# The delta rule's diagonal blocks inverted whole on GpSimd, in a fused transformer block and gMLP mixer

## Chip, cores and metric

One core of a Trainium2 chip. The metric is the device time of one execution in microseconds; of several executions, the median. The engines: TensorE (PE) multiplies, VectorE (DVE), ScalarE (ACT) and GpSimd (POOL) work element by element, and SyncE (SP) issues the transfers. TensorE writes to PSUM banks, the other data lie in SBUF.

## What is computed

Batch 1, 256 tokens, width 2048, all in float32. The first block has a modulation by `w_ada`, an input projection, a latent attention of 8 heads, a gated delta rule of 8 heads of 128, output projections and a gated feed-forward part of width 5632. A second block is a gMLP mixer of width 4096, with a norm at the end. The change is in the delta rule, which the reference computes in chunks of 64 tokens:

```python
kb = k * beta[..., None]
Lmat = jnp.where(strict, jnp.einsum('bhncd,bhnsd->bhncs', kb, k) * decay, 0.0)
A = Lmat + jnp.eye(CHUNK, dtype=jnp.float32)
rhs = jnp.concatenate([v * beta[..., None], kb * jnp.exp(G)[..., None]], axis=-1)
sol = lax.linalg.triangular_solve(A, rhs, left_side=True, lower=True, unit_diagonal=True)
```

The solution gives `u` and `w`; a scan over the chunks carries the state S of each head and yields the outputs. The kernel takes chunks of 128 tokens, so there are two for each head, and it needs to apply the inverse of a unit lower triangular matrix of 128 x 128 for each head and chunk.

## The kernel before

**A list of slots.** `Schedule` writes one list of steps, and each engine's program goes through that list and issues its own part, in order. The products of the weights are jobs of 512 output columns: TensorE consumes their weights in halves of two blocks of 128 rows, 12 products of 128x512 each, because every weight is split into a high and a low part (`hi` by ScalarE's cast, line 1528, `lo` by DVE's subtraction, line 2080) and each product is made of three. A half needs a place in SBUF for its two parts; four places serve this section (`NHL`), and a place is free once TensorE has consumed the half in it (`free_place`, `fill`). After each half `slot()` lets every background generator take one step. So a generator that yields n times spreads its steps over n slots.

**The section around the change.** It is the list of jobs `b`: for each c of 4 the pair `ga` (8 halves) and `om` (4), then `z` (2 jobs of 8) and `gb` (4 of 8). Beside them the remaining rows of `w_ada` come in by the units of `BESIDE`, and DVE reduces them, one row sum of 128x1024 each (line 2067). In this section `cells()` starts the delta rule: `prepare` for two chunks (tt) and two groups of four heads (g), then `invert`, then `solve(0, g)` and behind it `solve(1, g)`, then `gdn_final`. `build()` asks after the jobs of `b` for `("ogdn", 1, 1)`, the last transposes of `gdn_final`; if they had not been reached, slots without products would follow. In the list of before, the old inversion starts in slot 76 (`inv_in`), its eight slots of steps are 77 to 84, `inv_x` and `inv_out` stand in 85 and 86, the cells in 88 to 119, the last `og_t` in 132, and the last half of `gb` in 143. A step stands in front of the half of its slot: slot 90 opens with the first `ZT`, then comes its half.

**The inversion.** The strictly lower part of each 128x128 matrix (`Lm`, transposed) has four diagonal blocks of 32, each again of two by two blocks of 16. ScalarE picks the diagonal blocks (`gdn_pick`, line 1715) into `LP`. On DVE, `inv_in` (line 2293) transposes blocks of 32x32, and keeps for each partition the 16 entries of its own block of 16 (`LB`, with `bm2` as masks). `inv` (lines 2308 and 2311) does 15 steps j, a product and an addition over (15-j) x (j+1) columns each, all 128 partitions at once: the 16x16 blocks inverted. `inv_x` on ScalarE (line 1723) spreads them with the masks in two forms, `inv_out` (line 2316) transposes both back: `XO[0]` and `XO[1]`, the block inverses X and their transposes XT. Every one of these waits on semaphore `inv` or `gdn_pick`.

**The cells.** `dve_cell` in step X spreads the blocks into `X` and `XT` (line 2579), and for chunk 0 scales k (line 2613). Then TensorE multiplies `Lm` with `XT` (step ZT, four products of 128x128 in fp32 by `each`, line 1445), DVE masks the result with `pair` (line 2616), TensorE multiplies `X` with it (XZ), and DVE adds it to `XT` (line 2621): now XT holds the transposed inverses of the 32x32 blocks. Step NT multiplies once more and masks with `off`; U, NU, NW and NY apply the rest of the inverse. X, ZT, XZ and NT take two slots each.

**GpSimd** has nothing but powers: `power` (line 2669) forms x to the -0.5 for the norms, on 1, 2 or 4 columns. Each waits for its argument from DVE (line 1964).

Of the kernel before, what the change touches and what calls it, by code (L numbers as in the profile page):

```python
# [21 lines left out]
C_ID, C_ONE, C_INV, C_NH, C_COL, C_POS, C_C, C_TRI, C_PAIR = 0, 128, 256, 288, 296, 552, 554, 576, 704  # L22
C_OFF, C_CM, C_BM, C_ID16, C_AL, C_DT, C_GN, C_END = 832, 960, 1088, 1096, 1352, 1360, 1368, 1496
# [6 lines left out]
def shape_constants():  # L30
    i = np.arange(P)
    row, col = i[:, None], i[None, :]
    c = np.zeros((P, C_END), np.float32)
    c[:, C_ID:C_ID + P] = np.eye(P)
    c[:, C_ONE:C_ONE + P] = 1.0
    c[:, C_TRI:C_TRI + P] = row <= col
    c[:, C_PAIR:C_PAIR + P] = (row // 32 == col // 32) & (row % 32 < 16) & (col % 32 >= 16)
# [119 lines left out]
class Layout:  # L157


    def __init__(self, nc):  # L160
# [29 lines left out]
        self.pair, self.off, self.bm2 = C[:, C_PAIR:C_PAIR + P], C[:, C_OFF:C_OFF + P], C[:, C_BM:C_BM + 2]  # L190
# [62 lines left out]
        def pairs(kb):  # L253
            return ar(kb, 512).rearrange("p (j b n) -> p j b n", b=2, n=16)
        self.LP, self.LT = pairs(40), pairs(42)
        self.LB, self.XB, self.XP = (ar(kb, 256).rearrange("p (i j) -> p i j", j=16) for kb in (44, 45, 46))
        self.XE = [pairs(48), pairs(50)]
        self.XO = [ar(kb, 512).rearrange("p (n c) -> p n c", c=32) for kb in (12, 14)]
# [71 lines left out]
GATES = {"gta": 32, "gtf": 80}  # L330

# [5 lines left out]
class Schedule:  # L337
# [545 lines left out]
    def invert(self):  # L883
        while not {("prep", tt, g) for tt in range(2) for g in range(2)} <= self.have:
            yield
        yield
        self.put("inv_in")
        yield
        for j in range(0, 15, 2):
            self.put("inv", j, j + 2)  # L890
            yield
        self.put("inv_x")
        yield
        self.put("inv_out")
# [177 lines left out]
def cell_values(part, tt):  # L1072
    if part == 0:
        return (["kT", "qT", "KK", "AT"], ["d", "dm", "L", "Lb", "at", "atm"], ["kT", "exp", "qT"])
    if tt == 0:
        return (["ZT", "XZ", "NT", "U", "NU", "NW", "NY", "o", "S"],
                ["X", "XT", "kd", "ZT", "R", "XT2", "NT", "W", "V", "S", "ss", "n1", "n2"], ["U", "Y", "o", "sq"])
    return (["ZT", "XZ", "NT", "kS", "qS", "U", "NU", "NW", "NY", "o"],
            ["X", "XT", "ZT", "XT2", "NT", "R1", "R2", "R3", "QS", "W", "V", "o", "ss", "n1", "n2"], ["U", "Y", "sq"])
# [342 lines left out]
def pe_cell(e, L, S, W, held, args):  # L1422
# [42 lines left out]
    elif name == "ZT":  # L1465
# [37 lines left out]
def act_program(e, L, S, sch):  # L1503
# [3 lines left out]
    for step in sch.steps:  # L1507
# [200 lines left out]
        elif kind == "gdn_pick":  # L1708
# [249 lines left out]
def dve_program(e, L, S, sch):  # L1958
# [74 lines left out]
    for step in sch.steps:  # L2033
# [256 lines left out]
        elif kind == "inv_in":  # L2290
            W.wait_ge("gdn_pick", 16)
            W.wait_ge("cst_in", 32)
            e.transpose(L.LT.rearrange("p j b n -> p (j b n)"), L.LP.rearrange("p j b n -> p (j b n)")).then_inc(S["inv"], 1)
            lb = L.LB.rearrange("p i j -> p j i")
            W.wait_ge("inv", 1)
            e.tensor_scalar(lb, L.LT[:, :, 0, :], L.bm2[:, 0:1], None, ALU.mult).then_inc(S["inv"], 1)
            e.tensor_tensor(L.XB, L.CID, L.CID, ALU.mult).then_inc(S["inv"], 1)
            W.wait_ge("inv", 2)
            e.scalar_tensor_tensor(out=lb, in0=L.LT[:, :, 1, :], scalar=L.bm2[:, 1:2], in1=lb, op0=ALU.mult, op1=ALU.add
                                   ).then_inc(S["inv"], 1)  # L2300

        elif kind == "inv":
            j0, j1 = args
            for j in range(j0, min(j1, 15)):
                rows, shape = L.XB[:, j + 1:16, 0:j + 1], [P, 15 - j, j + 1]
                t = L.XP[:, 0:15 - j, 0:j + 1]
                W.wait_ge("inv", 2 * j + 4)
                e.tensor_tensor(t, L.LB[:, j + 1:16, j:j + 1].to_broadcast(shape),
                                L.XB[:, j:j + 1, 0:j + 1].to_broadcast(shape), ALU.mult).then_inc(S["inv"], 1)
                W.wait_ge("inv", 2 * j + 5)  # L2310
                e.tensor_tensor(rows, rows, t, ALU.add).then_inc(S["inv"], 1)
# [246 lines left out]
def dve_cell(e, L, S, W, args, mean_eps):  # L2558
# [104 lines left out]
def pool_program(e, L, S, sch):  # L2663
# [7 lines left out]
    for step in sch.steps:  # L2671
# [201 lines left out]
```

## Time and profile before

| | us |
|---|---|
| median of 3 runs | 2217.33 |
| lowest, highest | 2216.49, 2218.11 |
| profiled execution, first to last instruction | 2215.9 |
| PE busy in it | 2178.7 |
| DVE busy | 1499.2 |
| ACT busy | 1004.1 |
| POOL busy | 25.4 |

No time of its own beyond the span is listed for the profiled execution; the median is 1.4 us above that span. The granted clock of TensorE is 0.995 of full speed over the span and 1.00 in the windows of the section. Busy times of PE are modelled: a product of 128x512 is shown with 0.39 us, though the next one starts 0.23 us behind it, so starts are compared, not durations. On DVE consecutive records overlap by about 0.08 us. Idle time stands in brackets with what ended it. The lines named are those of the kernel before.

### The profile page before, as it was taken

Reading aid. Unit: us, or ns where it says so; the run is one execution under the profiler, and the core shown is the slowest. Engines: PE = TensorE matmul, PEld = TensorE weight load, DVE = VectorE, ACT = ScalarE, POOL = GpSimd, SP = SyncE. Lnnn points to the kernel's source line nnn. Section 1 sums busy time; section 2 is a strip of 40 time slices with the busy share of each in tenths; the row PEclk is TensorE's granted clock in tenths of the full one; section 3 lists DMA queues with packets and bytes.
Section 4 is the critical chain, followed back from the end, with each engine's and each line's share of the span. In section 5 each row is a group of like instructions: output and inputs, shape, how many; then the busy total and the mean of one; then the engine's idle time right before and its main releaser. Section 6 shows DMA issues by size and latency. Waiting matters only on the chain.

```text
span 2215.9 us, 27209 instructions
## 1 busy us (share of the span) xinstructions
PE 2178.7 (98%) x10552; PEld 1830.3 (83%) x10552; DVE 1499.2 (68%) x1881; ACT 1004.1 (45%) x1286; POOL 25.4 (1%) x26
## 2 busy tenths in 40 slices
PE   6899999999999999999999999999999999999998
PEld 5789988888888888888888888888888888888887
DVE  8988698988888677755455555575546555655556
ACT  5357455433444644443444334465444444444444
POOL 0001000000000000000000000000000000000000
PEclk9999999999999999999999999999999999999999
DMA  9975568977998688866666666666666666666663
GB/s 404 420 275 166 186 220 279 305 244 245 331 337 302 207 277 292 295 219 191 192 191 186 191 197 190 187 203 192 190 197 185 191 194 191 189 192 189 194 190 128
DMA packets 241552, 507.08 MB, mean 229 GB/s; under 512 B 19304, under 2 KB 34960, under 8 KB 235920
## 3 DMA queue, kind: packets, MB, share of 16 engines
q1 hardware_dynamic: 241424, 505.35, 70.2%
q8 instruction: 83, 1.36, 0.2%
q14 instruction: 45, 0.37, 0.0%
HBM read 503.16 MB, written 2.12 MB: 228 GB/s over the span
## 4 chain that ended last, share of the span: by engine, by line
PE 86%; DVE 6%; DMA 4%; ACT 2%; issue 2%; POOL 0%; DVEq 0%; ACTq 0%; POOLq 0%
PE bank L1254 25%; PE bank L1256 25%; PE bank L1255 25%; DVE WL L2080 2%; PE bank L1445 2%; PE bank L1186 2%; PE bank L1261 1%; PE bank L1263 1%; PE bank L1262 1%; DVE RAW L2067 1%; ACT WH L1528 1%; DMA RAW<-in_w_cd_dram 1%; DMA RAW<-in_w_ada_dram 1%; DMA A<-in_w_cq_dram 1%; DMA RAW<-in_w_cq_dram 1%
## 5 line engine op out<-in xcount | busy, mean ns | idle before, releaser
L2080 DVE TENSOR_TENSOR WL<-RAW,WH 128x1024 fp32r<-128x1024 f32 x706 | 859.9, 1222 | 576.7 <-ACT WH L1528 567.3
L1528 ACT CAST WH<-RAW 128x1024 fp32r<-128x1024 f32 x706 | 738.4, 1049 | 849.1 <-PE bank L1256 702.0
L1254 PE MATMUL bank<-WH,HTh 128*128 128x512 f32 x1922 | 758.1, 394 | 1.1 <-DVE WL L2080 1.0
L1256 PE MATMUL bank<-WH,HTl 128*128 128x512 f32 x1922 | 749.1, 390 | 0.0
L1255 PE MATMUL bank<-WL,HTh 128*128 128x512 f32 x1922 | 748.4, 389 | 0.0
L1256 PEld LDWEIGHTS bank<-WH,HTl 128*128 128x128 f32 x1922 | 360.8, 188 | 76.2
L1254 PEld LDWEIGHTS bank<-WH,HTh 128*128 128x128 f32 x1922 | 361.1, 188 | 75.7 <-DVE WL L2080 2.4
L1255 PEld LDWEIGHTS bank<-WL,HTh 128*128 128x128 f32 x1922 | 361.2, 188 | 72.2
L1254 PE MATMUL bank<-WH,R2h 128*128 128x512 f32 x408 | 160.6, 394 | 0.3 <-DVE WL L2080 0.3
L1256 PE MATMUL bank<-WH,R2l 128*128 128x512 f32 x408 | 159.0, 390 | 0.0
L1255 PE MATMUL bank<-WL,R2h 128*128 128x512 f32 x408 | 158.9, 389 | 0.0
L1254 PE MATMUL bank<-WH,aTh 128*128 128x512 f32 x344 | 134.1, 390 | 0.0
L1256 PE MATMUL bank<-WH,aTl 128*128 128x512 f32 x344 | 133.9, 389 | 0.0
L1255 PE MATMUL bank<-WL,aTh 128*128 128x512 f32 x344 | 133.8, 389 | 0.0
L2067 DVE CUSTOM_DVE_ANT_0 RAW<-RAW,CB,CST 128x1024 f32<-128x1024 f32 (+1 forms) x79 | 116.8, 1479 | 0.3
L1254 PEld LDWEIGHTS bank<-WH,R2h 128*128 128x128 f32 x408 | 76.6, 188 | 16.2 <-DVE WL L2080 0.8
L1256 PEld LDWEIGHTS bank<-WH,R2l 128*128 128x128 f32 x408 | 76.6, 188 | 16.1
L1255 PEld LDWEIGHTS bank<-WL,R2h 128*128 128x128 f32 x408 | 76.7, 188 | 15.4
L1261 PE MATMUL bank<-HTh,WH 128*128 128x256 f32 x308 | 89.4, 290 | 0.0
L1263 PE MATMUL bank<-HTh,WL 128*128 128x256 f32 x308 | 87.1, 283 | 0.0
L1262 PE MATMUL bank<-HTl,WH 128*128 128x256 f32 x308 | 87.1, 283 | 0.0
L2067 DVE CUSTOM_DVE_ANT_0 RAW<-RAW,CB,MOD 128x1024 f32<-128x1024 f32 x64 | 81.7, 1277 | 0.0
(302 smaller groups left out, 1823.5 us busy)
## 6 DMA issues: line engine op xcount, KB each, us to landing
RAW<-in_a_w_in_dram SPq DMA_DIRECT2D x192, 512.0 KB, 4.2
RAW<-in_w_gate_up_dram SPq DMA_DIRECT2D x176, 512.0 KB, 4.5
RAW<-in_w_ada_dram SPq DMA_DIRECT2D x128, 512.0 KB, 5.5
RAW<-in_w_in_dram SPq DMA_DIRECT2D x112, 512.0 KB, 4.8
RAW<-in_w_down_dram SPq DMA_DIRECT2D x88, 512.0 KB, 4.3
RAW<-in_a_w_out_dram SPq DMA_DIRECT2D x64, 512.0 KB, 4.1
A<-in_w_ada_dram SPq DMA_DIRECT2D x17, 1024.0 KB, 14.0
RAW<-in_w_o_dram SPq DMA_DIRECT2D x32, 512.0 KB, 5.9
```

What stands on the lines that cost most here:

```text
L1186: t = e.transpose(dst[:, i * P:(i + 1) * P], s, ident)
L1254: e.matmul(o, ah[:, s], hi[:, k, :], start=first, stop=False)
L1255: e.matmul(o, ah[:, s], lo[:, k, :], start=False, stop=False)
L1256: i = e.matmul(o, al[:, s], hi[:, k, :], start=False, stop=last)
L1261: e.matmul(o, hi[:, k, s], ah, start=first and cb % 2 == 0, stop=False, skip_group_check=True)
L1262: e.matmul(o, hi[:, k, s], al, start=False, stop=False, skip_group_check=True)
L1263: i = e.matmul(o, lo[:, k, s], ah, start=False, stop=last, skip_group_check=True)
L1445: i = e.matmul(dst[:, h, :], left[:, h, :], right[:, h, :], start=True, stop=True)
L1528: e.copy(hi, rv).then_inc(S["hi"], 1)
L2067: e.tensor_tensor_reduce(out=rv, in0=rv, in1=L.CB[:, w], scale=0.5, scalar=first[:, col:col + 1], op0=ALU.mult, op1=ALU.add, accum_out=L.M ...
L2080: e.tensor_tensor(lo, rv, hi.bitcast(F32), ALU.subtract).then_inc(S["lo"], 1)
```

## The change

The diagonal blocks of 32 are inverted whole, in 31 steps over up to 16 columns a partition (the two halves of a block's columns lie in different partitions), and GpSimd does these steps instead of DVE. `inv` now has 62 instructions, each waiting for the one before. For them there are 13 slots (`INV_STEPS`) and six empty ones. The steps ZT and XZ with their products, masks and additions are gone, and so is the block form `XO[0]`: step X spreads only `XT`. `v` is scaled in step X. The inversion runs through larger picks and transposes, and `XO` is the sum of the two halves of `XF`. The constant `pair` is gone, which makes the constants 128 columns shorter.

```diff
+INV_STEPS = [(0, 3), (3, 6)] + [(j, j + 2) for j in range(6, 24, 2)] + [(24, 27), (27, 31)]
@@ invert
-        for j in range(0, 15, 2):
-            self.put("inv", j, j + 2)
+        for j0, j1 in INV_STEPS:
+            self.put("inv", j0, j1)
+            yield
+        for _ in range(6):
             yield
@@ solve
-        for name in ("X", "ZT", "XZ", "NT") + ("kS",) * tt + ("U", "NU", "NW", "NY", "o"):
+        for name in ("X", "NT") + ("kS",) * tt + ("U", "NU", "NW", "NY", "o"):
             at(name)
             yield
-            if name in ("X", "ZT", "XZ", "NT"):
+            if name in ("X", "NT"):
                 yield
@@ pe_cell
-    elif name == "ZT":
+    elif name == "NT":
         for n in (na, nb):
             for other, value in held[n]:
                 W.wait_ge(other, value)
         W.wait_ge(dve, d("XT"))
-        each(a, Lm, XT).then_inc(mine, 1)
-    elif name == "XZ":
-        W.wait_ge(dve, d("ZT"))
-        each(b, X, q).then_inc(mine, 1)
-    elif name == "NT":
-        W.wait_ge(dve, d("XT2"))
         each(a, Lm, XT).then_inc(mine, 1)
@@ act_program
                 e.copy(L.LP[r, :, :, n:n + 4].rearrange("p j b h -> p h b j"),
-                       lm[r, :, r].rearrange("p h (b j) -> p h b j", j=16)).then_inc(S["gdn_pick"], 1)
+                       lm[r, :, r].unsqueeze(2).to_broadcast([32, 4, 2, 32])).then_inc(S["gdn_pick"], 1)
         elif kind == "inv_x":
-            W.wait_ge("inv", 34)
-            for n in range(2):
-                src = L.XB if n else L.XB.rearrange("p i j -> p j i")
-                for b in range(2):
-                    e.activation(L.XE[n][:, :, b, :], src, ACT.Copy, scale=L.bm2[:, b:b + 1]).then_inc(S["gdn_pick"], 1)
+            W.wait_ge("inv", 65)
+            for b in range(2):
+                e.activation(L.XE[:, :, b, :], L.XB, ACT.Copy, scale=L.bm2[:, b:b + 1]).then_inc(S["gdn_pick"], 1)
@@ dve_program
-            e.transpose(L.LT.rearrange("p j b n -> p (j b n)"), L.LP.rearrange("p j b n -> p (j b n)")).then_inc(S["inv"], 1)
...
+            e.transpose(L.LT.rearrange("p j i -> p (j i)"), L.LP.rearrange("p j b n -> p (j b n)")).then_inc(S["inv"], 1)
+            for b in range(2):
+                e.tensor_scalar(L.XB[:, 16 * b:16 * b + 16, :], L.CID, L.bm2[:, b:b + 1], None, ALU.mult).then_inc(S["inv"], 1)
         elif kind == "inv_out":
-            for n in range(2):
-                W.wait_ge("gdn_pick", 2 * n + 18)
-                e.transpose(L.XO[n].rearrange("p n (b j) -> p j b n", b=2), L.XE[n]
-                            ).then_inc(S["inv"], 1)
+            W.wait_ge("gdn_pick", 18)
+            e.transpose(L.XF.rearrange("p i b n -> p (i b n)"), L.XE.rearrange("p i b c -> p (i b c)")).then_inc(S["inv"], 1)
+            W.wait_ge("inv", 66)
+            e.tensor_tensor(L.XO.rearrange("p n i -> p i n"), L.XF[:, :, 0, :], L.XF[:, :, 1, :], ALU.add).then_inc(S["inv"], 1)
@@ dve_cell
-        spread_blocks(X, L.XO[0])
-        spread_blocks(XT, L.XO[1])
+        spread_blocks(XT, L.XO)
         if tt == 0:
             e.tensor_tensor(k, k, bc4(L.eD[:, 0, hs]), ALU.mult).then_inc(mine, 1)
-    elif name == "ZT":
-        W.wait_ge(pe, m("ZT"))
-        e.tensor_tensor(q, a, bm4(L.pair), ALU.mult).then_inc(mine, 1)
-        if tt == 0:
             e.tensor_tensor(v, v, bc4(L.beta[:, 0, hs]), ALU.mult).then_inc(mine, 1)
-    elif name == "XZ":
-        W.wait_ge(pe, m("XZ"))
-        e.tensor_tensor(XT, XT, b, ALU.add).then_inc(mine, 1)
@@ pool_program
+        elif kind == "inv":
+            for j in range(*args):
+                n, w = 31 - j, min(j + 1, 16)
+                rows, t, shape = L.XB[:, j + 1:32, 0:w], L.XP.rearrange("p i c -> p (i c)")[:, 0:n * w], [P, n, w]
+                t = t.rearrange("p (i c) -> p i c", c=w)
+                W.wait_ge("inv", 2 * j + 3)
+                e.tensor_tensor(t, L.LT[:, j, j + 1:32].unsqueeze(2).to_broadcast(shape),
+                                L.XB[:, j:j + 1, 0:w].to_broadcast(shape), ALU.mult).then_inc(S["inv"], 1)
+                W.wait_ge("inv", 2 * j + 4)
+                e.tensor_tensor(rows, rows, t, ALU.add).then_inc(S["inv"], 1)
```

## Rows read from the trace of the kernel before

**Rows 1.** The page: span, busy time by engine (us, share), chain by engine.
```profile
span 2215.9 us, 27209 instructions
...
PE 2178.7 (98%) x10552; PEld 1830.3 (83%) x10552; DVE 1499.2 (68%) x1881; ACT 1004.1 (45%) x1286; POOL 25.4 (1%) x26
...
PE 86%; DVE 6%; DMA 4%; ACT 2%; issue 2%; POOL 0%; DVEq 0%; ACTq 0%; POOLq 0%
```

**Rows 2.** Windows: us, then busy us (instructions) by engine, clock, DMA share, GB/s.
```profile
390.00:400.00 10.00, 10.00 (x46) 8.29 (x45) 9.96 (x16) 4.26 (x6) 0.00 (x0) 1.00 0.86 272
410.00:420.00 10.00, 10.00 (x46) 8.29 (x45) 9.62 (x23) 3.96 (x4) 0.00 (x0) 1.00 1.01 355
420.00:430.00 10.00, 9.92 (x44) 7.87 (x44) 9.97 (x16) 6.35 (x9) 0.00 (x0) 1.00 0.91 301
430.00:440.00 10.00, 9.46 (x50) 7.80 (x49) 10.00 (x15) 3.00 (x3) 0.00 (x0) 1.00 0.83 284
```

**Rows 3.** Timeline of PE: start us, us, engine, line, operation, count [idle before].
```profile
432.71 0.39 PE L1256 MATMUL bank<-WH,HTl 128*128 128x512 f32 x1
432.94 0.39 PE L1254 MATMUL bank<-WH,HTh 128*128 128x512 f32 x1
...
434.32 1.13 PE L1445 MATMUL bank<-A 128*128 128x128 f32 x8 [0.54 <-DVE A L2579]
...
437.80 0.39 PE L1256 MATMUL bank<-WH,HTl 128*128 128x512 f32 x1
438.02 1.05 PE L1445 MATMUL bank<-A 128*128 128x128 f32 x8
438.83 0.48 PE L1254 MATMUL bank<-WH,HTh 128*128 128x512 f32 x1
439.15 0.40 PE L1255 MATMUL bank<-WL,HTh 128*128 128x512 f32 x1
```

**Rows 4.** Timeline of DVE, first and last step of the old inversion.
```profile
397.09 0.70 DVE L2293 STREAM_TRANSPOSE A<-A 128x512 f32<-128x512 f32 x1
...
427.49 2.11 DVE L2316 STREAM_TRANSPOSE A<-A 128x512 f32<-128x512 f32 x2
```

**Rows 5.** Lines of DVE, 399 to 448.5: count | busy us, mean ns.
```profile
L2080 DVE TENSOR_TENSOR WL<-RAW,WH 128x1024 fp32r<-128x1024 f32 x16 | 19.5, 1216 | 0.0
...
L2579 DVE TENSOR_TENSOR A<-A,CST 128x512 f32<-128x512 f32 x4 | 2.6, 681 | 0.0
...
L2311 DVE TENSOR_TENSOR A<-A 128x63 f32<-128x63 f32 x2 | 0.5, 225 | 0.1
```

**Rows 6.** Timeline of POOL, powers of one and four columns.
```profile
485.98 1.95 POOL L2669 TENSOR_TENSOR ST<-ST,CST 128x4 f32<-128x4 f32 x1 [4.84 <-DVE ST L1964]
543.10 1.01 POOL L2669 TENSOR_TENSOR ST<-ST,CST 128x4 f32<-128x4 f32 x1 [55.17 <-DVE ST L1964]
...
745.37 0.55 POOL L2669 TENSOR_TENSOR ST<-ST,CST 128x1 f32<-128x1 f32 x1 [195.26 <-DVE ST L1964]
```

**Rows 7.** Timeline of DVE beside the power at 485.98.
```profile
485.84 1.22 DVE L2080 TENSOR_TENSOR WL<-RAW,WH 128x1024 fp32r<-128x1024 f32 x1
```

**Rows 8.** Timeline of both engines, 304 to 307.
```profile
304.05 2.70 POOL L2669 TENSOR_TENSOR ST<-ST,CST 128x4 f32<-128x4 f32 x2 [93.13 <-DVE ST L1964]
...
304.67 1.22 DVE L2264 SCALAR_TENSOR_TENSOR A<-A 128x1024 f32<-128x1024 f32 x1
...
305.81 1.28 DVE L2067 CUSTOM_DVE_ANT_0 RAW<-RAW,CB,MOD 128x1024 f32<-128x1024 f32 x1
...
307.01 1.22 DVE L2080 TENSOR_TENSOR WL<-RAW,WH 128x1024 fp32r<-128x1024 f32 x1
```

**Rows 9.** Lines of ACT, 399 to 448.5: count | busy us, mean ns | idle before.
```profile
L1528 ACT CAST WH<-RAW 128x1024 fp32r<-128x1024 f32 x16 | 16.7, 1050 | 26.5 <-DMA RAW<-in_w_o_mla_dram 18.5 <-DMA RAW<-in_w_in_dram 8.1
L1723 ACT ACTIVATE A<-A,CST 128x256 f32<-128x256 f32 x4 | 2.2, 622 | 1.6 <-DVE A L2311 1.6
L1747 ACT ACTIVATE A<-bank 128x512 f32<-128x512 f32 x4 | 2.2, 591 | 0.1
```

More of the change, by code:

```diff
@@ L20 @@
 KB = 256
-C_ID, C_ONE, C_INV, C_NH, C_COL, C_POS, C_C, C_TRI, C_PAIR = 0, 128, 256, 288, 296, 552, 554, 576, 704
-C_OFF, C_CM, C_BM, C_ID16, C_AL, C_DT, C_GN, C_END = 832, 960, 1088, 1096, 1352, 1360, 1368, 1496
+C_ID, C_ONE, C_INV, C_NH, C_COL, C_POS, C_C, C_TRI = 0, 128, 256, 288, 296, 552, 554, 576
+C_OFF, C_CM, C_BM, C_ID16, C_AL, C_DT, C_GN, C_END = 704, 832, 960, 968, 1224, 1232, 1240, 1368
 CS = 3 * P + 80
@@ L36, in shape_constants @@
     c[:, C_TRI:C_TRI + P] = row <= col
-    c[:, C_PAIR:C_PAIR + P] = (row // 32 == col // 32) & (row % 32 < 16) & (col % 32 >= 16)
     c[:, C_OFF:C_OFF + P] = row // 32 < col // 32
@@ L189, in __init__ @@
         self.CID = C[:, C_ID16:C_ID16 + 256].rearrange("p (i j) -> p i j", j=16)
-        self.pair, self.off, self.bm2 = C[:, C_PAIR:C_PAIR + P], C[:, C_OFF:C_OFF + P], C[:, C_BM:C_BM + 2]
+        self.off, self.bm2 = C[:, C_OFF:C_OFF + P], C[:, C_BM:C_BM + 2]
         self.bm4 = C[:, C_BM + 2:C_BM + 6]
@@ L252, in __init__ @@
         self.SS = [ar(96, 512).rearrange("p (h d) -> p h d", d=P), ar(98, 512).rearrange("p (h d) -> p h d", d=P)]
[L253 to L258, printed above, removed]
+        self.LP = ar(40, 1024).rearrange("p (j b n) -> p j b n", b=2, n=16)
+        self.LT = ar(44, 1024).rearrange("p (j i) -> p j i", i=32)
+        self.XB, self.XP = (ar(kb, w).rearrange("p (i c) -> p i c", c=16) for kb, w in ((48, 512), (50, 256)))
+        self.XE = ar(52, 1024).rearrange("p (i b c) -> p i b c", b=2, c=16)
+        self.XF = ar(40, 1024).rearrange("p (i b n) -> p i b n", b=2, n=16)
+        self.XO = ar(12, 512).rearrange("p (n i) -> p n i", i=32)
         self.cell = [[ar(64 + 16 * g + 2 * i, 512).rearrange("p (h d) -> p h d", d=P) for i in range(8)] for g in range(2)]
@@ L1075, in cell_values @@
     if tt == 0:
[L1076 to L1079, printed above, removed]
+        return (["NT", "U", "NU", "NW", "NY", "o", "S"],
+                ["XT", "kd", "R", "NT", "W", "V", "S", "ss", "n1", "n2"], ["U", "Y", "o", "sq"])
+    return (["NT", "kS", "qS", "U", "NU", "NW", "NY", "o"],
+            ["XT", "NT", "R1", "R2", "R3", "QS", "W", "V", "o", "ss", "n1", "n2"], ["U", "Y", "sq"])
 def count_cells():
@@ L2292, in dve_program @@
             W.wait_ge("cst_in", 32)
-            e.transpose(L.LT.rearrange("p j b n -> p (j b n)"), L.LP.rearrange("p j b n -> p (j b n)")).then_inc(S["inv"], 1)
[L2294 to L2299, printed above, removed]
-                                   ).then_inc(S["inv"], 1)
[L2302 to L2311, printed above, removed]
+            e.transpose(L.LT.rearrange("p j i -> p (j i)"), L.LP.rearrange("p j b n -> p (j b n)")).then_inc(S["inv"], 1)
+            for b in range(2):
+                e.tensor_scalar(L.XB[:, 16 * b:16 * b + 16, :], L.CID, L.bm2[:, b:b + 1], None, ALU.mult).then_inc(S["inv"], 1)
         elif kind == "inv_out":
-            for n in range(2):
-                W.wait_ge("gdn_pick", 2 * n + 18)
-                e.transpose(L.XO[n].rearrange("p n (b j) -> p j b n", b=2), L.XE[n]
-                            ).then_inc(S["inv"], 1)
+            W.wait_ge("gdn_pick", 18)
+            e.transpose(L.XF.rearrange("p i b n -> p (i b n)"), L.XE.rearrange("p i b c -> p (i b c)")).then_inc(S["inv"], 1)
+            W.wait_ge("inv", 66)
+            e.tensor_tensor(L.XO.rearrange("p n i -> p i n"), L.XF[:, :, 0, :], L.XF[:, :, 1, :], ALU.add).then_inc(S["inv"], 1)
         elif kind == "z":
@@ L2607, in dve_cell @@
     elif name == "X":
-        W.wait_ge("inv", 36)
+        W.wait_ge("inv", 67)
         W.wait_ge(own, CELL["dve", 1, "atm"] if tt == 0 else CELL["dve", 0, "n2"])
-        spread_blocks(X, L.XO[0])
-        spread_blocks(XT, L.XO[1])
+        spread_blocks(XT, L.XO)
         if tt == 0:
             e.tensor_tensor(k, k, bc4(L.eD[:, 0, hs]), ALU.mult).then_inc(mine, 1)
-    elif name == "ZT":
-        W.wait_ge(pe, m("ZT"))
-        e.tensor_tensor(q, a, bm4(L.pair), ALU.mult).then_inc(mine, 1)
-        if tt == 0:
             e.tensor_tensor(v, v, bc4(L.beta[:, 0, hs]), ALU.mult).then_inc(mine, 1)
-    elif name == "XZ":
-        W.wait_ge(pe, m("XZ"))
-        e.tensor_tensor(XT, XT, b, ALU.add).then_inc(mine, 1)
     elif name == "NT":
```

## The prediction, before the changed kernel was timed

> **What bounds the kernel now.** I read the page first. TensorE is busy for 2178.7 of the 2215.9 us of the span and holds 86% of the chain that ended last, and VectorE (DVE) is second [rows 1]. So what comes off TensorE's queue comes off the time, and what makes TensorE wait is added. GpSimd (POOL) is free: 25.4 us in the whole span. Then I read the windows around the inversion, which DVE's timeline starts at 397.09 [rows 4]. There DVE is full too: 9.6 to 10 us of every 10 from 390 to 440, with TensorE losing only 0.08 and 0.54 us between 420 and 440 [rows 2]. The program is a list of slots; in each, TensorE consumes one half of weights, 12 products. In TensorE's timeline they start 0.227 us apart (432.71 to 432.94, rounded) [rows 3], so a slot is 2.72 us of TensorE. Counting the schedule, the old inversion begins in slot 76 and its `inv_out` stands in slot 86; DVE takes 30.4 us for these ten slots (397.09 to 427.49) [rows 4] where TensorE needs 27.2. DVE's lead is eaten here, and only four halves can be prepared ahead.
>
> All costs come from one profiled execution of 2215.9 us span. No time of its own outside the span is listed; the runs' median is 2217.33, 1.4 us more, and I carry differences over to that median. A measurement of this kernel can tell about 0.2% (4.4 us) from no change.
>
> **TensorE, removed.** `ZT` and `XZ` each issue four products in fp32, 8 records, for each of four cells: eight groups. From a product at 437.80, the next one after such a group starts at 438.83 instead of 438.02: 0.81 us. The first product behind it then takes 0.32 us to its successor (438.83 to 439.15) instead of 0.227: 0.09 more [rows 3]. Eight times 0.90 is **7.2 us**. They stand alone in their slots, so the switch is paid for each. The wait of 0.54 us in front of the first group (434.32, behind the spreading of X) [rows 3] and the 0.08 us before it [rows 2] come from DVE being late; with DVE relieved I take **0.6 us** as gone. Together 7.8 us, 2209.5, if nothing else waits.
>
> **Slots.** The inversion gets 13 slots of steps and 6 empty ones for 8: eleven more. Each cell drops four, and two cells follow one another: eight fewer. The last cell transposes move from slot 132 to 135, and the section ends with slot 143, so no slot without products appears: 0 us, covered by 12 slots of slack (past it, each extra one would be a bubble of the chain's length).
>
> **DVE.** Gone are 30 small operations of up to 0.225 us (at most 6.8 us), and in the four cells a spread, a mask and an addition of 0.68 each (8.2 us) [rows 5]. The doubled block transpose in front costs 0.7 us more; behind, one of twice the width plus an addition takes the place of two of together 2.11 us [rows 4]: even. All of it lies beside TensorE; it is only worth the 0.6 us above. **ScalarE**: the 16 picks copy 256 instead of 128 values; `inv_x` is two operations of 512 columns for four of 0.62 us [rows 9]. The first costs less than 0.2 us each, beside ScalarE's waits for DMA (26.5 us of idle time in 49.5) [rows 9]: 0; without that cover 3 us. Constants: 64 KB less in one early transfer, 0.
>
> **GpSimd, added.** 62 dependent products and additions with 9552 columns in all (the sum of (31-j) times min(j+1,16), twice). No row shows one of them. The nearest on the same engine are powers: 0.55 us for one column, 1.01 for four [rows 6], thus 0.40 fixed and 0.153 per column. The nearest of the same kind is DVE's: 0.682 for 512 columns, 1.216 for 1024 [rows 5], 1.04 ns a column. So 62 x 0.40 = 24.5 us (DVE's own fixed part, 0.15 us, would give 9), and for the columns between 9.9 us and, at the power's rate, 1461 us. A multiplication is one pass and no power, so I stay near DVE's row; since POOL's fixed part is 2.6 times DVE's, I take twice its rate, 2.06 ns, 19.7 us. Alone the chain takes **44.2 us**. The Trainium skill (GPSIMD Engine Reference, Performance versus the Vector engine) has 4497 ns for 2048 columns; by that, an estimate from the page, the columns come to 21 us and nothing else changes.
>
> **Does it fit?** DVE ends the new `inv_in` near 399.2 (1.4 us of transposing, then two small ones). `inv_x` opens slot 96 on ScalarE, behind the cast of slot 95. The group that opened slot 90 could start at 433.6 without its wait; the place which that cast fills comes free five halves later, 433.6 + 5 x 2.72 = 447.2, and the cast of 1.05 us [rows 9] ends at 448.2. That gives 49 us. Alone, POOL ends at 443.4: in time, by 5 us.
>
> But POOL isn't alone. A power of four columns takes 1.01 us beside a DVE operation with one input in SBUF, and 1.95 when it starts (485.98) behind a DVE subtraction with both inputs in SBUF (485.84, 1.22 us): it ends 0.87 us after that one [rows 6, 7]. The same pair stands at 548. In [rows 8] the second of two powers runs only behind 304.67 + 1.22 and ends 0.86 us later, though DVE's next operation had already begun: POOL gets in between two of them, once. The Trainium skill (SBUF — State Buffer, Who interferes with whom) says that such a DVE instruction and a GpSimd instruction that reads SBUF exclude each other, the later one waiting to the end; the trace agrees (1.95 against 1.01).
>
> In the 49 us DVE does 18 splits, which hold it for 1.14 us each (304.67 to 305.81, an operation of the same 1.22), and, by the units planned beside these jobs, 15 row sums of `ada`, 1.20 each (305.81 to 307.01) [rows 8]: 38.5 us with both inputs in SBUF, 78%. The open 11 us are about what the readings at the seams take (33 x 0.32). So POOL does about one instruction per DVE instruction, 34 of 62, until 448.2. The last 28 (columns 17 to 30) have 3360 columns: 11.1 + 6.9 = 18 us, now unhindered, since DVE soon waits for ScalarE, which waits at `inv_x`. POOL ends at **466.5**.
>
> **What is queued behind.** Behind `inv_x` on ScalarE stand the casts, behind them DVE's splits, and TensorE has four more halves ready, until 433.6 + 9 x 2.72 = 458.1. The next one is there at 466.5 + 1.2 (`inv_x`, 2 x 0.59) + 1.05 + 1.22 = 470.0: TensorE stands for 11.9 us. With no lead left, DVE then needs 4.4 us for the next slot (`inv_out` 2.1, a row sum, a split) against 2.72, and 3.8 in each slot that begins a cell (three operations of 0.68 less 0.08 of overlap, a split, three quarters of a row sum): 1.7 + 2.2. The stall is **15.8 us**, the sum -7.2 - 0.6 + 15.8 = **+8.0 us: 2225.3**.
>
> **Rivals.**
> A. The chain fits (faster). If POOL and DVE pass each other more easily than [rows 7] say, or POOL's fixed part is DVE's, it ends before 454.7 (458.1 - 3.4), which is 0.90 us per instruction. Then only the 7.8 us count: 2209.5. For it: alone it needs 0.71 us each. Against: both stretched powers. Chance 0.33. With 3.9 us of catching up behind it, break-even is a stall of 7.8 us, at 0.96 us each.
> B. Half a lock (even). If `ada`'s row sums don't hold POOL up (no row shows that they do), only 20 of the 49 us are closed; POOL ends between 455 and 462, the stall is 3 to 11 us: 2213 to 2221. Chance 0.13.
> C. DVE is held too, for as long as POOL reads. 34 instructions with 6192 columns x 2.06 ns would add 12.8 us to DVE's 41 (38.5 and two evictions of two operations) in those 49 us, 4.6 us too much: 2230; with twice the time per column, 6.9 us more behind the window and some in it, about 2240. For it: one shared way in works both ways. Against: no DVE operation in the rows is stretched (those powers read only a few columns). Chance 0.19. The Trainium skill (SBUF — State Buffer, Who interferes with whom) states this direction too; no row shows it.
> D. Multiplications cost what powers do: over 3600 us. Chance 0.01.
> Forecast: 0.34.
>
> **How the numbers follow.** Faster by over 0.2%: A, and a sliver of B: 0.34. Within: the rest of B, 0.13. Slower: forecast, C and D, 0.53. The range runs from just under A (2208.5) to the upper end of C (2240). The forecast's own range is 2221 to 2230.
>
> **What would show it.** L1445 with 64 fewer records. POOL at some 40 to 60 us busy from 399 on, its operations stretched where they meet L2080 and L2067; DVE rows of these lines longer than 1.22 and 1.28 would be C. Idle time of ScalarE at `inv_x` behind POOL, and TensorE idle for 10 to 20 us between 455 and 490. If POOL ends before 450 and TensorE has no such gap, the step of the shared way was wrong and A holds.

## The result, and the profile after

The changed kernel takes **2221.93 us** (median of 10 runs, 2221.51 to 2223.48) against 2217.16 (10 runs, 2215.79 to 2218.11): the ratio is 1.0022, interval 1.0015 to 1.003, thus 4.8 us slower (3.3 to 6.6). Forecast were 2225.3 and a range of 2208.5 to 2240. The page of the profile after, against [rows 1]:

```profile
span 2221.4 us, 27098 instructions
...
PE 2174.5 (98%) x10488; PEld 1825.4 (82%) x10488; DVE 1497.9 (67%) x1838; ACT 1011.4 (46%) x1284; POOL 86.6 (4%) x88
...
PE 86%; DVE 5%; DMA 3%; POOL 3%; ACT 2%; issue 1%; DVEq 0%; ACTq 0%; POOLq 0%
```

TensorE has 64 records and 4.2 us of work less, and yet the span is 5.5 us longer. GpSimd works 61.2 us more, and it now has 3% of the chain that ended last, where it had nothing. The windows around the inversion, with the columns of [rows 2], show where TensorE's gain was given back:

```profile
430.00:440.00 10.00, 10.00 (x46) 8.29 (x45) 10.00 (x10) 2.12 (x2) 9.53 (x7) 1.00 0.90 306
440.00:450.00 10.00, 9.99 (x45) 7.94 (x44) 10.00 (x11) 5.20 (x6) 9.53 (x7) 1.00 0.99 354
450.00:460.00 10.00, 8.37 (x36) 6.56 (x36) 7.16 (x9) 1.05 (x1) 9.14 (x12) 1.00 0.94 319
460.00:470.00 10.00, 0.77 (x2) 0.67 (x3) 2.05 (x2) 4.42 (x6) 4.45 (x15) 0.68 0.04 15
470.00:480.00 10.00, 10.00 (x42) 8.19 (x41) 9.97 (x14) 1.76 (x2) 0.00 (x0) 0.81 0.70 221
```

Between 430 and 440 TensorE no longer loses the 0.54 us of [rows 2]; between 460 and 470 it does next to nothing, and the granted clock is 0.68. Who waited for whom between 390 and 560 (waiter, releaser: us in total, times, longest us):

```profile
ACT A L1717 <- POOL A L2670: 14.3, 1, 14.3
...
PE bank L1256 <- DVE WL L2074: 10.9, 1, 10.9
...
DVE WL L2074 <- ACT WH L1524: 15.6, 6, 10.8
...
PE bank L1447 <- DVE A L2603: 0.7, 1, 0.7
```

So it is the forecast's queue: GpSimd's last addition (L2670) releases `inv_x` on ScalarE (L1717), the cast behind it (L1524) releases DVE's split (L2074), and that releases TensorE. The same chain in the timelines of GpSimd, ScalarE and DVE:

```profile
399.64 1.15 POOL L2667 TENSOR_TENSOR A<-A 128x31 f32<-128x31 f32 x1 [92.72 <-DVE A L2289]
...
420.97 0.57 POOL L2667 TENSOR_TENSOR A<-A 128x220 f32<-128x220 f32 x1
...
439.27 1.49 POOL L2667 TENSOR_TENSOR A<-A 128x256 f32<-128x256 f32 x1
...
440.83 1.60 POOL L2670 TENSOR_TENSOR A<-A 128x256 f32<-128x256 f32 x1
...
458.16 0.43 POOL L2667 TENSOR_TENSOR A<-A 128x144 f32<-128x144 f32 x1
...
465.33 0.22 POOL L2670 TENSOR_TENSOR A<-A 128x16 f32<-128x16 f32 x1
```

```profile
450.26 1.05 ACT L1524 CAST WH<-RAW 128x1024 fp32r<-128x1024 f32 x1 [1.56 <-DMA RAW<-in_w_in_dram]
465.58 1.34 ACT L1717 ACTIVATE A<-A,CST 128x512 f32<-128x512 f32 x2 [14.27 <-POOL A L2670]
466.82 3.88 ACT L1524 CAST WH<-RAW 128x1024 fp32r<-128x1024 f32 x4
```

```profile
420.34 1.27 DVE L2328 SCALAR_TENSOR_TENSOR A<-A,bank 128x512 f32<-128x512 f32 x2
...
438.57 1.70 DVE L2074 TENSOR_TENSOR WL<-RAW,WH 128x1024 fp32r<-128x1024 f32 x1
440.20 1.64 DVE L2061 CUSTOM_DVE_ANT_0 RAW<-RAW,CB,MOD 128x1024 f32<-128x1024 f32 x1
...
467.95 1.23 DVE L2074 TENSOR_TENSOR WL<-RAW,WH 128x1024 fp32r<-128x1024 f32 x1 [10.79 <-ACT WH L1524]
469.10 1.24 DVE L2293 STREAM_TRANSPOSE A<-A 128x1024 f32<-128x1024 f32 x1
470.37 1.07 DVE L2295 TENSOR_TENSOR A<-A 128x512 f32<-128x512 f32 x1
```

From 399.64 to 465.55 are 65.9 us for 62 dependent instructions. The first, of 31 columns, takes 1.15 us. The two of 256 columns at 439.27 and 440.83 take 1.49 and 1.60 us and start 1.56 us apart, beside DVE operations of 1.70 and 1.64 us that start 1.63 apart: the two engines go at one pace, while the same two DVE operations take 1.22 and 1.28 where nothing meets them. Later (458.16), with DVE waiting for ScalarE, a product of 144 columns takes 0.43 us. Nor does every DVE operation hold GpSimd up: beside L2328 (420.34), which reads one of its inputs from a bank in PSUM, the product of 220 columns at 420.97 takes 0.57 us, and beside the same line at 454.33 a product of 176 columns takes 0.48 (454.95), which is its length alone (445.90 in the first run below). TensorE's timeline:

```profile
457.99 0.39 PE L1258 MATMUL bank<-WH,HTl 128*128 128x512 f32 x1
469.23 0.79 PE L1256 MATMUL bank<-WH,HTh 128*128 128x512 f32 x1 [10.86 <-DVE WL L2074]
469.82 0.63 PE L1257 MATMUL bank<-WL,HTh 128*128 128x512 f32 x1
470.25 0.63 PE L1258 MATMUL bank<-WH,HTl 128*128 128x512 f32 x1
...
474.00 0.39 PE L1258 MATMUL bank<-WH,HTl 128*128 128x512 f32 x1
474.24 0.39 PE L1256 MATMUL bank<-WH,HTh 128*128 128x512 f32 x1
```

It would have gone on at 458.2 (457.99 + 0.227) and does so at 469.23: 11.0 us. The 12 products of this half then take until 474.24, 5.0 us instead of 2.72. They start 0.43 us apart (469.82 to 470.25), 1.9 times the 0.227 of full speed, which is the level of 1.2 GHz; from 474.00 on they are back at 0.24. The low clock costs 2.3 us more.

### The profile page after: what moved, and what is told of

Same layout as the page of the kernel before. It is cut to its first block, busy times and chain, and to the rows that moved or that the text cites. A ratio compares the mean times of both kernels' runs of the same rounds, so it can differ in the third digit from the quotient of the medians.

```text
span 2221.4 us, 27098 instructions
## 1 busy us (share of the span) xinstructions
PE 2174.5 (98%) x10488; PEld 1825.4 (82%) x10488; DVE 1497.9 (67%) x1838; ACT 1011.4 (46%) x1284; POOL 86.6 (4%) x88
## 3 DMA queue, kind: packets, MB, share of 16 engines
q8 instruction: 83, 1.36, 0.2%
## 4 chain that ended last, share of the span: by engine, by line
PE 86%; DVE 5%; DMA 3%; POOL 3%; ACT 2%; issue 1%; DVEq 0%; ACTq 0%; POOLq 0%
PE bank L1256 26%; PE bank L1258 26%; PE bank L1257 25%; DVE WL L2074 2%; PE bank L1188 2%; POOL A L2670 1%; PE bank L1263 1%; PE bank L1265 1%; PE bank L1264 1%; POOL A L2667 1%; PE bank L1447 1%; DVE RAW L2061 1%; ACT WH L1524 1%; DMA RAW<-in_w_cd_dram 1%; DMA RAW<-in_w_ada_dram 1%
## 5 line engine op out<-in xcount | busy, mean ns | idle before, releaser
L2074 DVE TENSOR_TENSOR WL<-RAW,WH 128x1024 fp32r<-128x1024 f32 x706 | 866.5, 1232 | 584.6 <-ACT WH L1524 576.8
L1524 ACT CAST WH<-RAW 128x1024 fp32r<-128x1024 f32 x706 | 741.5, 1054 | 833.6 <-PE bank L1258 684.6
```

Source lines behind the costliest of these rows:

```text
L1524: e.copy(hi, rv).then_inc(S["hi"], 1)
L2074: e.tensor_tensor(lo, rv, hi.bitcast(F32), ALU.subtract).then_inc(S["lo"], 1)
```

## The experiments

Two theories stood against each other at first. **P**: the shared way of the forecast (one GpSimd instruction per two-input DVE operation). **Q**: GpSimd's instructions are slow in themselves. Then came the questions of what removes the stall, and what the removed products were worth. Each time stands beside that of the kernel before, timed together with it; "ends" is the end of GpSimd's last addition.

**1 to 3: how many slots are kept for the chain.** The changed kernel has `range(6)`.

```diff
-        for _ in range(6):
+        for _ in range(0):    # e1; 10 in e2, 13 in e3
```

> The changed kernel with none of the six empty slots. ScalarE then reaches inv_x six slots (16.3 us of TensorE) earlier, near 435 instead of 451.3, and TensorE runs dry near 442 instead of 458.2. Theory P (GpSimd is held up by DVE's operations with two inputs in SBUF, and runs free once DVE stands): about 35 of the 62 instructions are still to do at 436, with some 4860 columns; at the free rate of the changed kernel's rows (0.27 us each and 1.7 ns a column) they take 18 us, the chain ends near 455 instead of 465.5, the stall grows only from 11 to about 16 us: 2227.5 us. Rival Q (GpSimd's own pace, DVE has no part): the chain ends at 465.5 as before, the stall grows by the whole 16.3 us: 2238 us.

> The changed kernel with ten empty slots instead of six; TensorE needs the next half 10.9 us later, near 469. Rival Q (GpSimd's own pace): the chain ends at 465.5, its followers 3.7 us later, so TensorE hardly waits: 2210 us, all of the 7.8 us gained. Theory P (held up by DVE): DVE goes on for four more slots, the tail of the chain that ran free now meets it too, at 1.1 to 1.4 us an instruction; the chain ends between 467 and 470, and a stall of 2 to 5 us with its low clock remains: 2212 to 2215 us.

> Thirteen empty slots; the last cell transposes then stand in slot 142, just ahead of the end of the section in 143. Both theories: no stall is left, since even with every instruction held up (62 times 1.4 us at most, less for the short ones) the chain ends before TensorE needs its half near 477. 2209 to 2211 us: the eight groups of products (7.2 us) and the small waits, so this run prices the removed products. If TensorE's gain was less than 0.9 us a group, it shows here.

| slots kept | ends (us) | TensorE's wait (us) | time, before (us) | ratio (interval) |
|---|---|---|---|---|
| 0 | 455.6 | 18.4 | 2230.02, 2217.53 | 1.0057 (1.0043 to 1.0071) |
| 6 (the change) | 465.6 | 10.9 | 2221.93, 2217.16 | 1.0022 (1.0015 to 1.003) |
| 10 | 472.7 | 6.9 | 2218.91, 2217.53 | 1.0007 (0.9998 to 1.0016) |
| 13 | 476.2 | 2.9 + 1.1 | 2215.89, 2217.53 | 0.9992 (0.9983 to 1.0) |

GpSimd's timeline without the slots:

```profile
434.32 1.48 POOL L2667 TENSOR_TENSOR A<-A 128x252 f32<-128x252 f32 x1
...
435.88 1.55 POOL L2670 TENSOR_TENSOR A<-A 128x252 f32<-128x252 f32 x1
...
438.99 0.62 POOL L2667 TENSOR_TENSOR A<-A 128x256 f32<-128x256 f32 x1
...
439.69 0.74 POOL L2670 TENSOR_TENSOR A<-A 128x256 f32<-128x256 f32 x1
...
455.42 0.22 POOL L2670 TENSOR_TENSOR A<-A 128x16 f32<-128x16 f32 x1
```

With `inv_x` earlier in its queue, DVE runs out of splits earlier (its last operation before the stall starts at 436.81), GpSimd is alone from 437.5 on, and its operations fall from 1.55 to 0.62 and 0.74 us. The chain ends 10 us earlier at the same count and size of instructions, so P holds and Q does not. The end was expected near 455 and came at 455.6; the stall of 18.4 us was expected at about 16, and the time is 2.5 us over the 2227.5 expected. The stall is longer than with six slots, since TensorE ran dry earlier. More slots are each worth less than the 2.72 us of TensorE that they give, because the chain gets longer in them. In the run with ten:

```profile
464.04 1.36 POOL L2670 TENSOR_TENSOR A<-A 128x144 f32<-128x144 f32 x1
...
466.81 0.46 POOL L2670 TENSOR_TENSOR A<-A 128x128 f32<-128x128 f32 x1
...
472.44 0.22 POOL L2670 TENSOR_TENSOR A<-A 128x16 f32<-128x16 f32 x1
```

Even the addition of 144 columns is still held to 1.36 us; it goes free only at 466.8. From 0 to 6, 10 and 13 slots the end moves by 10.0, 7.1 and 3.5 us, for 16.3, 10.9 and 8.2 us of TensorE's work. My expectations for ten and thirteen failed: the times came 4 to 7 us later, since they let the tail run free, and for thirteen slots they had no stall at all. They also left out the clock. TensorE with thirteen slots:

```profile
479.90 0.50 PE L1256 MATMUL bank<-WH,HTh 128*128 128x512 f32 x1 [2.93 <-DVE WL L2074]
...
480.99 0.63 PE L1256 MATMUL bank<-WH,HTh 128*128 128x512 f32 x1
481.42 0.63 PE L1257 MATMUL bank<-WL,HTh 128*128 128x512 f32 x1
```

After a wait of only 2.9 us products again start 0.43 us apart, and the 12 of this half take 4.4 us instead of 2.72 (the last one starts at 484.11): 1.7 us more. With ten slots it is 2.0 us (476.38 to 481.06) behind a wait of 6.9, with six 2.3 behind 11.0. So the price of the low clock hardly followed the length of the wait in these three runs. For thirteen slots the terms are 7.9 us gained (below), 4.0 of waits and 1.7 of clock: 2.2 us faster, and 1.6 was measured.

**4: the same inversion on DVE.** The block `inv` goes from `pool_program` to `dve_program`, its 62 operations unchanged.

```diff
@@ pool_program
-        elif kind == "inv":
@@ dve_program
+        elif kind == "inv":
```

> The changed kernel, but VectorE does the 62 steps itself, in the same slots. GpSimd has nothing. VectorE's own cost is 62 times 0.2 us and 9552 columns at 1.04 ns: 22 us more work for it in 19 slots (52 us of TensorE), where it has about 44 us already: 66 against 52, less a lead of 4 us: TensorE waits for about 8 to 10 us, in small pieces: 2218 to 2221 us. If the chain on GpSimd cost nothing but its own time, this would be the slower one; if sharing the way in costs DVE as much as doing the work (its operations grew from 1.22 to 1.7 us), they are about equal.

2221.01 us (before 2217.53), 1.0017 (1.0008 to 1.0026): at the upper end of what was expected, and within the intervals the same as on GpSimd (1.0022, 1.0015 to 1.003). In DVE's timeline a step of 256 columns takes 0.42 us, less than on GpSimd alone (0.62 and 0.74):

```profile
422.67 0.42 DVE L2297 TENSOR_TENSOR A<-A 128x256 f32<-128x256 f32 x1
```

The time is lost in another way, mostly in small waits of TensorE (380 to 600: waiter, releaser, total, times, longest):

```profile
PE bank L1256 <- DVE WL L2074: 7.6, 7, 2.1
```

Between 400 and 450 TensorE is busy for 43.14 us of 50 here, where the changed kernel has 49.99. So with these slots handing the chain to the idle engine bought nothing over leaving it on DVE: there its 62 operations make DVE late in many places, on GpSimd they make one long wait. DVE's version with fewer empty slots was not tried; it may not need the six.

**5 and 6: columns or count.** Both leave out a part of the inversion, so their results are not the inverse, and each was timed once. The first leaves out half of the columns of each step; the second leaves out all 31 additions.

```diff
# e5
-                n, w = 31 - j, min(j + 1, 16)
+                n, w = 31 - j, (min(j + 1, 16) + 1) // 2
# e6 (waits of inv: j + 3, 34, 35, 36)
-                W.wait_ge("inv", 2 * j + 4)
-                e.tensor_tensor(rows, rows, t, ALU.add).then_inc(S["inv"], 1)
```

> The changed kernel, each of the 62 GpSimd instructions on about half the columns (4968 instead of 9552 in all; the other half is left out). Theory P (each instruction waits for one DVE operation with two inputs in SBUF, so their count sets the end): the middle ones shrink only by their own reading, from 1.55 to 1.35 us, and the chain ends near 459 instead of 465.5. DVE's splits beside them, 1.70 us with full columns, shrink to about 1.45, halfway to 1.22. Rival (the columns set the end): 66 us become about 40, the chain ends near 440.

> The changed kernel without the 31 additions on GpSimd (they are left out, so the chain has 31 instructions with 4776 columns, about as many columns as the run before it). Theory P: 31 instructions at 1.35 us end near 441, some 18 us before the chain with half the columns. Rival (columns set the end): both end at the same time, near 440. TensorE has no stall here in either case: about 2210 to 2212 us, and the profile shows what is left of the gain when only DVE's slower operations remain.

Both leave GpSimd about half of the 9552 columns (4968 and 4776). With half the width the chain runs from 397.9 to 455.4, 57.5 us (its end was expected near 459), TensorE still waits once for 2.5 us, and the kernel takes 2212.74 us (before 2217.38). GpSimd, and the DVE operation beside it:

```profile
431.37 1.27 POOL L2667 TENSOR_TENSOR A<-A 128x128 f32<-128x128 f32 x1
```

```profile
433.65 1.46 DVE L2074 TENSOR_TENSOR WL<-RAW,WH 128x1024 fp32r<-128x1024 f32 x1
```

With half the instructions it takes 41.7 us and ends at 439.2 (expected near 441), with no stall, 2208.13 us (expected 2210 to 2212). The group of all 31 in GpSimd's timeline:

```profile
397.49 41.73 POOL L2667 TENSOR_TENSOR A<-A 128x31 f32<-128x31 f32 x31 [91.98 <-DVE A L2289]
```

At equal columns the count makes 16 us of difference, 1.35 us per instruction against 0.93. Halving the columns took 8.4 us off the 65.9, halving the count 24.2. The number of turns weighs most, as P says; the columns count too, since they make each turn longer. The split's length follows the columns beside it: 1.22 us beside none, 1.46 beside 128, 1.70 beside 255.

**7: what the removed products were worth.** The kernel before gets eight more groups of four products, in the slots behind the steps ZT and NT.

```diff
+                if name in ("ZT", "NT"):
+                    at("more")
...
+    elif name == "more":
+        each(b, Lm, XT)
```

> The kernel before, with one more group of four products of 128x128 alone in each of eight slots, into a bank that is free (its result isn't used). It prices the removed products: eight groups at 0.90 us are 7.2 us: 2224.7 us. If a group cost only the 0.53 us that its eight records would take at the pace of the big products in columns, it would be 2221.5 us; if TensorE had room, 2217.5.

2223.39 us against 2217.38, 1.003 (1.0018 to 1.0041): 6.0 us (4.0 to 9.1), 7.2 expected. TensorE's timeline shows two groups back to back:

```profile
437.52 0.39 PE L1258 MATMUL bank<-WH,HTl 128*128 128x512 f32 x1
...
437.75 1.95 PE L1447 MATMUL bank<-A 128*128 128x128 f32 x16
...
439.45 0.48 PE L1256 MATMUL bank<-WH,HTh 128*128 128x512 f32 x1
```

From 437.75 to 439.45 are 1.70 us for two groups where [rows 3] have 0.81 for one: the second adds 0.89. Eight are 7.1 us. The expectation was wrong in one thing: none of the eight stands alone in its slot, each joins a group that was there. So the run prices a second group (0.89), and the price of one that stands alone, as the removed ones did, remains that of [rows 3] (0.81 + 0.09); the two are equal to 0.01 us. The time agrees, but by itself it can't tell them from the rival of 0.53 us a group (4.2 us), which lies in its interval too; the rows can.

**8 to 10: fewer row sums beside the chain.** If DVE's operations make GpSimd's turns long, row sums of `ada` that stand elsewhere should shorten it. In the eighth run those of `om` 2, `om` 3 and `ga` 3 stand behind the inversion; in the ninth eight of them stand ahead of it, with ten slots; the tenth is the kernel before with the ninth's plan.

```diff
# e8, in BESIDE
-("om", 2): (0, 1, 2, 3), ("om", 3): (0, 1, 2, 3), ("ga", 3): (1, 2, 3, 5, 7)
+("om", 2): (), ("om", 3): (), ("ga", 3): (), ("z", 1): tuple(range(8)), ("og", 0): (0, 1, 2, 3)
+("gb", 0): tuple(range(8)), ...
# e9 and e10, in BESIDE
+("om", 2): (1, 3), ("om", 3): (1, 3), ("ga", 3): (3,), ("conv", 3): (0, 1, 3, 5, 7)
+("ukk", 0): (1,), ("ukk", 1): (1,), ("ukv", 0): (0, 1), ("ukv", 1): (0, 1)
```

> The changed kernel with its six slots, but the 13 pairs of loads and row sums of w_ada that stand beside om 2, ga 3 and om 3 are planned later, beside z 1, gb and og 0. DVE then has one split a slot and no row sum in most of the inversion. Theory P: GpSimd gets about three instructions into a slot of 2.72 us instead of two, the chain ends between 446 and 456 instead of 465.5, in time for TensorE (454.5): no stall or one under 2 us, and 2209 to 2213 us, if z, gb and og bear the denser loads. Rival (GpSimd's own pace, or a count of its waits that has nothing to do with the row sums): it still ends near 465 and the stall of 11 us stays: 2220 us.

> The changed kernel with ten empty slots, and eight of the 13 row sums beside om 2, ga 3 and om 3 (with their loads) planned earlier, beside ukk, ukv and conv 3, where DVE has 4 to 8 us of every 20 idle and DMA is half idle. Theory P: with half the row sums gone GpSimd gets in more often than with ten slots alone (end 472.4) and less often than without any (452.9): the chain ends between 458 and 466, TensorE needs it by 465.4: a stall of 0 to 1 us. With a ceiling of 9 us (the run of half the count had no stall and 2208.1): 2208 to 2211 us, faster than both kernels. If the early section doesn't bear the loads, TensorE waits there before 390 and the gain is less: up to 2215.

> The kernel before, with the same eight row sums planned earlier: the control for the run before it. DVE is relieved where it is full, but TensorE lost only 0.6 us there: 2216 to 2218 us. If this run gained as much as the one before, the gain would be the plan's and not the inversion's.

The eighth took 2219.03 us (before 2217.38), 1.0007 (0.9998 to 1.0016). Its chain ends at 452.9, within the 446 to 456 expected, and the stall is gone; TensorE waits once for 1.5 us. GpSimd's operations (this kernel's lines are one further on):

```profile
424.83 0.63 POOL L2668 TENSOR_TENSOR A<-A 128x255 f32<-128x255 f32 x1
...
425.54 1.65 POOL L2671 TENSOR_TENSOR A<-A 128x255 f32<-128x255 f32 x1
...
427.26 0.62 POOL L2668 TENSOR_TENSOR A<-A 128x256 f32<-128x256 f32 x1
...
427.96 0.74 POOL L2671 TENSOR_TENSOR A<-A 128x256 f32<-128x256 f32 x1
```

Three of these four are free, and the whole chain needs 55 us (397.76 to 452.93) instead of 65.9. But the time missed its expectation (2209 to 2213) by 6 us: what was moved costs elsewhere. Between 600 and 650 TensorE is busy for 47.24 of 50 us, where the kernel before had 50.00. For 2.5 of the 2.8 us it waits for the row sums themselves, whose results it needs there (`MOD`) and which now come too late:

```profile
600.00:650.00 50.00, 47.24 (x211) 37.95 (x210) 45.06 (x58) 21.10 (x24) 0.00 (x0) 1.00 1.03 386
```

```profile
PE bank L1389 <- DVE MOD L2062: 2.5, 2, 2.0
```

Another 2.7 us are two waits of TensorE for DVE in the cells (L2604 and L2608, 1.9 and 0.8), where the changed kernel has one of 0.7.

Moved ahead (the ninth), they cost as much: 2218.25 us (before 2216.3), 1.0009 (1.0 to 1.0018), where 2208 to 2211 was expected. The chain is shorter (65.1 us, with ten slots alone 72.5), but it starts 7 us later, at 406.66, and ends at 471.8, not between 458 and 466. The tenth took 2222.63, 1.0028 (1.0017 to 1.0038), where 2216 to 2218 was expected: the plan alone costs 6.3 us. Between 200 and 300 TensorE is busy for 94.16 of 100 us in it, where the kernel before has 100.00, and between 150 and 390 it waits 4.9 us for DVE's splits. So the early section does not bear the load. Measured against the tenth run, the change with its ten slots gains 4.4 us. Neither of the two plans found a cheap place for the row sums; others were not tried.

**11 and 12: a version a little faster than both.** Thirteen slots, and DVE does the first three steps (six operations) itself right behind `inv_in`; the twelfth also moves two row sums from `ga` 3 to `conv` 3.

```diff
@@ dve_program, inv_in
+            for j in range(3):
...
@@ pool_program, inv
-            for j in range(*args):
+            for j in range(max(3, args[0]), args[1]):
# e12 only, in BESIDE
-("conv", 3): (1, 3, 5), ("ga", 3): (1, 2, 3, 5, 7)
+("conv", 3): (0, 1, 3, 5, 7), ("ga", 3): (1, 3, 7)
```

> Thirteen empty slots, and DVE does the first three steps itself right behind inv_in: six operations, which took GpSimd 5.8 us (399.6 to 405.4) and cost DVE about 1.5. Theory P: GpSimd starts its 56 instructions some 1.5 us later and still ends 3 to 4 us earlier than with thirteen slots alone (476.2), at 472 to 473.5; TensorE needs it by 473.5. The stall of 2.9 us and its successor of 1.1 go: 2211 to 2213.5 us, against 2215.9. If GpSimd only used the freed time to wait longer, it stays at 2215.9.

> The same, and two of the row sums beside ga 3 are planned beside conv 3 instead, where the windows from 250 to 300 showed no TensorE wait with them. Theory P: two fewer operations in GpSimd's way, the chain ends 1 to 2 us earlier still, no stall: 2210.5 to 2213 us. If conv 3 doesn't bear them, TensorE waits between 200 and 300 and this run is slower than the one before it.

The eleventh took 2215.06 us (before 2216.86), 0.9991 (0.9982 to 1.0), where 2211 to 2213.5 was expected. DVE's six operations lie between 398.20 and 399.7, 0.19 to 0.25 us each, where four of the six take GpSimd 1.15 us or more (two get in free, in 0.3), and the chain ends at 474.2 instead of 476.2. But the time is no better than with thirteen slots alone (0.9992): what the head start on DVE is worth can't be told from nothing. The twelfth took **2213.14**, 0.9985 (0.9976 to 0.9994), 3.7 us (1.3 to 5.3) faster than before, and 1.9 faster than the eleventh, from which only the two moved row sums set it apart. Its chain ends at 472.1, and TensorE still waits 2.7 us behind it, where none was expected:

```profile
481.52 0.50 PE L1256 MATMUL bank<-WH,HTh 128*128 128x512 f32 x1 [2.66 <-DVE WL L2074]
```

## Why the prediction was right

The likeliest case came true, by the mechanism written down; one of its numbers, the end of the chain, was helped by errors that cancel. Of its terms:

- **TensorE, removed.** 7.2 us forecast. Seventh run: 7.1 by its rows, 6.0 (4.0 to 9.1) by its time. The waits for the spreading of X are gone as said; they were 0.8 us, as a second one of 0.25 at 495.47 had not been counted.
- **The stall.** The mechanism is the one written down, link by link. The chain's end: 466.5 forecast, 465.55 measured. TensorE dry: 458.1 and 458.2. Back: 470.0 and 469.23. The stall itself: 11.9 and 11.0.
- **That the chain's end came out to 1 us is in part luck.** The first 34 instructions took 46.0 us (399.64 to 445.61), forecast 49. The last 28 took 19.9, forecast 18, and there two errors cancel: they were to run unhindered from 448.2, but DVE still had splits and row sums until 457.1 and held seven of the 28; and alone they cost 14 us by the rates of the first run, not 18.
- **The 3.9 us of catching up failed**, the step "with no lead left, DVE then needs 4.4 us for the next slot", against 2.72 of TensorE. DVE did need 4.5 us from one split to the next (467.95 to 472.48). But TensorE did not take 2.72: at its low clock the first half took 5.0 us, so the next split was there in time. Behind it DVE needed 2.3, 2.9 and 4.1 us from split to split, where TensorE, with the groups of NT between its halves, took 3.6 a slot. Only 0.7 us were lost in a later cell (L2603). In place of the 3.9 stand 2.3 us of low clock, which the sum had no term for and which is itself what hid the first part of them.
- **Alone, the chain was priced too high.** 44.2 us forecast. The free rows of the first run give 0.62 and 0.74 us for 256 columns and 0.22 for 16. An addition thus has (0.74 - 0.22)/240 = 2.17 ns a column and 0.22 - 16 x 0.00217 = 0.19 us fixed; a product, with the same fixed part, (0.62 - 0.19)/256 = 1.7 ns a column. Over the 62 that is 0.19 x 62 + 4776 x (1.7 + 2.17) ns = 30 us, and with 0.08 us between two of them 35. This is an estimate from three lengths. The fixed part of 0.40, taken from the powers of [rows 6], was too high (0.19, or 0.27 with the gap); the doubled rate for the columns was about right (2.06 forecast, 1.94 on average). For the held instructions the error did not count, since they take DVE's length and not their own.
- **Rival C was half true.** DVE is held as well: splits of 1.55 us on average (19 between 399 and 451) for 1.22, row sums of 1.55 and 1.49 (7 of each form) for 1.28, together some 9.6 us where C had 12.8. The Trainium skill (SBUF — State Buffer, Who interferes with whom) says that the lock works both ways; the trace agrees (1.70 against 1.22). But C's consequence did not come. ScalarE came to `inv_x` at 451.3 (the cast at 450.26 and its 1.05 us) instead of 448.2, 3 us late where C says 4.6. (That cast waited last for its load, 1.56 us, so how much of the 3 us is DVE's is not shown.) And the halves ahead of it, though later, were still there before TensorE wanted them: it ran dry at 458.2 as without C.
- **Rival B is false.** The row sums hold GpSimd up too: the one at 440.20 (1.64 us) stands beside an addition of 1.60 (alone 0.74), which ends 0.6 us behind it (442.43 against 441.84). **Rival A** failed with the lock: 1.06 us per instruction, where it needed 0.90. Alone the widest operations take 0.62 and 0.74 us (first run), and the 35 us of all 62 would fit; no run keeps all of DVE's two-input operations away, so that A would have held then is argued, not shown. **D** is false.
- **Slips in the sums.** 448.2 + 18 is 466.2, not 466.5; 62 x 0.40 is 24.8, not 24.5; and with D counted among the slower cases their chance is 0.54 and that of no difference 0.12. None changes the forecast by more than 0.3 us.

With the measured terms the sum is -7.1 (products) - 0.8 (waits gone) + 11.0 (stall) + 2.3 (clock) + 0.7 (later cell) = +6.1 us; 5.5 lie between the two spans, 4.8 (3.3 to 6.6) between the medians. The forecast of +8.0 had one term too many (3.9) and one too few (2.3).

## What to carry to other kernels

An engine that is 1% busy is not free if it shares a way with the busy one: count how many dependent instructions the moved work has, and price each at one operation of the neighbour plus a part for its own columns, as long as the neighbour is busy with operations that read two inputs from SBUF. Keeping more slots for such a chain also gives the neighbour more operations to hold it with, so each slot is worth less than its length (6 slots moved the end by 10 of 16.3 us). The fifth and sixth runs point to fewer and larger instructions as the first cure. Giving the neighbour the narrow first steps moved the chain's end by 2 us but no time that could be measured; taking two of its operations out of the chain's way was worth 1.9 us. And a wait of 3 us of TensorE is not a small thing: the low clock behind it cost 1.7 us more.

## What the runs showed of the hardware

- A dependent chain on GpSimd costs, alone, 0.19 us per instruction and 0.08 between two, and 1.7 (product) or 2.2 ns (addition) a column, an estimate from the lengths of 16 and 256 columns (0.22, and 0.62 or 0.74 us). The powers of [rows 6], at 0.40 us and 0.153 us a column, are no guide to it.
- Beside a GpSimd instruction of 256 columns a DVE operation of 1024 is longer by 0.4 to 0.5 us (1.22 to 1.70, 1.28 to 1.64), beside one of 128 columns by 0.24 (1.46). The two alternate one for one where DVE has no gap and the instruction has 144 columns (1.36 us held) or 31 (1.15). A DVE operation with one input in PSUM (L2328) did not hold GpSimd up: 0.57 us for 220 columns.
- After 11 us of idleness TensorE's granted clock stood at 0.68 and 0.81 in the two windows, and about ten products ran at the level of 1.2 GHz: 2.3 us on top of the stall. Behind waits of 6.9 and 2.9 us (ten and thirteen slots) the same level cost 2.0 and 1.7 us.
